# A hybrid decoder step on one core: split waits, moved copies, an earlier reload and a regrouped end

## The chip, the cores and the metric
The kernel runs on one core of one Trainium2 chip. A core has TensorE (PE, matrix products), VectorE (DVE), ScalarE (ACT), GpSimd (POOL), and SyncE (SP), which here only issues DMA transfers; 16 DMA engines move the data. The metric is the device time of one execution in microseconds (us).

## The reference
One layer of a decoder for 320 tokens: 256 of a prompt and 64 of 8 samples of 8. All is float32.

```python
h = rms_norm(x, g_mix)
proj = h @ w_in                  # u | qkv | z | beta | a | gate_a | gate_b
y_s5 = gelu(s5(u))               # diagonal complex state space, scan over positions
y_s5 = y_s5 * sigmoid(y_s5 @ w_glu + b_glu)
y_dn = gated_delta(conv(qkv), beta, a, S0) ; norm ; * silu(z)
mix = sigmoid(gate_a) * (y_s5 @ w_a) + sigmoid(gate_b) * (y_dn @ w_b)
x = x + mix @ w_out
x = x + (silu(h2 @ w_gate) * (h2 @ w_up)) @ w_down       # h2 = rms_norm(x, g_ffn)
x = x + (p @ w_ple) * sigmoid(h3 @ w_ple_gate)           # h3 = rms_norm(x, g_ple)
y = rms_norm(x, g_final)         # y_prompt 256 x 2048, y_sample 8 x 8 x 2048
```

D is 2048, the S5 and DeltaNet widths are 1024, FFN 5632, the per-layer embedding p has 256 columns. The states of the convolution, the DeltaNet and the S5 branch are outputs too.

## The kernel before
Activations lie transposed, features on the 128 partitions and the 320 tokens along the row. A weight is cut into units of 512 rows by 256 columns (512 KB). SP loads unit n into slot n mod 4 of the ring `raw` as soon as unit n-4 has been split; SP's queue is in order, so a load or store placed between two units waits for its own conditions with all later loads behind it. ScalarE rounds the unit to `whi` (L959), VectorE takes the rest `wlo` = raw - whi (L1410); the activations have halves of the same kind (`xhi`/`xlo`, for the S5 branch `yhi`/`ylo`). TensorE multiplies a unit in three parts of 8 products each: whi with the high half, whi with the low half, wlo with the high half (`unit`, L2172), into the accumulator `pg`.

What runs between the units is written out by hand. `schedule()` is a list of slots, each with side tasks and a number of units. Every engine walks the same list: TensorE does a slot's side tasks and then its units; ScalarE and VectorE split the slot's units first and then do the side tasks. So on ScalarE and VectorE a side task of one slot stands ahead of the splits of the next. Their PSUM results go to two regions, `side_a` and `side_b`, used in turn as `side_fills()` lists them.

Side tasks named below: `sq` h multiplies a sample's query and key with head h's old state (VectorE uses the result at L1900, `vb`); `vn` and `o` 2 belong to the sample's chunk; the decay of a head's state is L1660 (`st` times `egl`, 128x1024); `su` adds to the states; `ysplit` makes `yhi` on ScalarE (L1220) and `ylo` on VectorE (L1926). `masked_values(h)` makes 8 masked copies `vnb` on ScalarE (within L962) which `su` needs. After the gates come the products of the glu (`glu`, 4 pairs of 2 units), then w_a and w_b with the gates fetched back by SP from DRAM (`gr`, L590), then w_out.

The input x is written to DRAM early (`scratch_x`) and loaded back to `xt` (2560 KB, L621) ahead of w_out's residual addition. MIX_UNITS is the number of units before w_out.

Last comes the per-layer embedding: 8 rounds of four units of w_ple_gate and one of w_ple (256 rows), into `side_a` and `side_b` by turns (`emb` i). After round 7: gate, sigmoid (L1348), product `fmd` (L2092), addition to `xt` (L2100), squares (L1358), their sum in `acc`, and the column sums of `acc` with ones (`norm` 3, L2198) which give `invt`, one number per token. TensorE turns `xg` (xt times the norm's weight) to token-major by products with `ident` (L2646, L2660) in five groups: `fin` 0 0, `turned_0`, `turned_1`, `fin` 1 1 and `fin` 2 (the samples, two column halves on 2 x 64 partitions). ScalarE (L1389) and VectorE (L2141) scale them by `invt` into `yo` and `yo2`, and SP stores them (L655 to L664).

ScalarE's own DMA queue carries 11 small transfers in the first slot (`const`): four norm weights as 16 rows of 128, two vectors as 8 rows, one row, the convolution's 96 rows, and three tables of 32 rows:

```python
src = w if w is g_final else w[0]
act.dma_start(par1n[at:at + KD, :], src.rearrange("(k p) -> k p", p=P)).then_inc(sem("par_landed"), 16)
...
act.dma_start(par1n[ONW:ONW + 1, :], onorm_w).then_inc(sem("par_landed"), 16)
```

Of the kernel before, what the change touches and what calls it, by code (L numbers as in the profile page):

```python
# [22 lines left out]
P = 128  # L23
# [116 lines left out]
def schedule():  # L140
# [108 lines left out]
def hybrid_layer(nc, x_prompt, x_sample, state_conv, state_delta, state_s5_re, state_s5_im, p_prompt, p_sample,  # L249
# [26 lines left out]
    with ExitStack() as ctx:  # L276
# [189 lines left out]
        xg = zo.take("xg", [P, KD, NPR])  # L466
        xgs = zo.take("xgs", [P, KD // 2, 2, NSM])

        scr_x = nc.dram_tensor("scratch_x", [P, KD, N], F32, kind="Internal").ap()
# [68 lines left out]
        def _(sp):  # L538
# [54 lines left out]
            for n, (p, j) in enumerate(units):  # L593
# [24 lines left out]
            sp.wait_ge(sem("x_stored"), 16)  # L618
            sp.wait_ge(sem("on_ready"), H // 2)
            sp.wait_ge(sem("st_stored"), 16 * H)  # L620
            sp.dma_start(xt[:], scr_x).then_inc(sem("xt_landed"), 16)  # L621

# [328 lines left out]
        def _(act):  # L951
# [80 lines left out]
            def side(key):  # L1032
# [168 lines left out]
                elif what == "o":  # L1201
                    c0, n = CHUNKS[a[0]]
                    wait_filled(act, key)
                    drain(act.activation(hsplit(qt[:, :, c0:c0 + n]), hview(key, a[0]), ACT.Copy), key)
                    if a[0] == 2:
                        wait_drained(act, ("vn", 2))
                        masked_values(0)
                        masked_values(1)
                elif what == "sq":
                    if a[0] == 0:  # L1210
                        wait_filled(act, ("s", 1))
                    wait_filled(act, key)
                    copy(vn[NSM:P, a[0], :], ps(key)[NSM:P, 0, 0:P]).then_inc(sem("qs_ready"), 1)
                elif what == "su" and a[0] + 2 < H:
                    masked_values(a[0] + 2)
# [134 lines left out]
            def final_x(i):  # L1350
                act.wait_ge(sem("xf_ready"), i + 1)
                if i < 7:
                    finish(xt, i + 24, i, None)
                else:
                    act.wait_ge(sem("acc_added"), 31)
# [9 lines left out]
            for i in range(8):  # L1365
# [35 lines left out]
        def _(dve):  # L1401
# [260 lines left out]
            def side(key):  # L1662
# [231 lines left out]
                elif what == "sq":  # L1894
                    h = a[0]
                    if h == 0:
# [190 lines left out]
            def ple_out(i):  # L2087
# [5 lines left out]
                wait_drained(dve, key)  # L2093
                if i < 7:
                    xs = xt[:, 2 * i:2 * i + 2, :]
                    dve.tensor_tensor(xs, xs, fmd[:], ALU.add).then_inc(sem("xf_ready"), 1)
                    dve.wait_ge(sem("xf_ready"), i + 1)
                else:
                    for m in range(2):
                        dve.tensor_tensor(xt[:, 14 + m, :], xt[:, 14 + m, :], fmd[:, m, :], ALU.add).then_inc(sem("xf_ready"), 1)  # L2100

            dve.wait_ge(sem("phi_ready"), 1)
            dve.tensor_tensor(plo[:], pf[:], phi[:].bitcast(F32), ALU.subtract).then_inc(sem("plo_ready"), 1)
            for i in range(8):
# [15 lines left out]
                else:  # L2120
# [6 lines left out]
                    s(4)  # L2127
            ple_gate_out(7)
            ple_out(7)
# [20 lines left out]
        def _(pe):  # L2150
# [10 lines left out]
            def unit(u, r, par, k0, nk, first, last, hi, lo, out=None, lows_ready=None):  # L2161
# [12 lines left out]
                ins.then_inc(multiplied, 1)  # L2174

            def token_transposes(out, cols, src):

# [4 lines left out]
            def norm(i):  # L2182
                key = ("norm", i)
                if i == 3:
                    pe.wait_ge(sem("last_added"), 3)
                elif i:
# [9 lines left out]
                if i == 3:  # L2196
                    for c in range(3):
                        ins = pe.matmul(out[:, 1, c:c + 1], acc[:, c * P:(c + 1) * P], ones[:, 0:1], start=True, stop=True)  # L2198
                end(ins, key)
# [350 lines left out]
            for s, (sides, us) in enumerate(slots):  # L2550
                for key in sides:
                    side(key)
                for n in [units.index(u) for u in us]:
# [77 lines left out]
            for i in range(KD // 2):  # L2631
# [6 lines left out]
                out = begin(key)  # L2638
                unit(u + 4, (5 * i + 4) % RING, None, 0, PLE // P, True, True, phi, plo, out)
                if i == 0:  # L2640
# [13 lines left out]
            pe.wait_ge(evacuated, PLE_P + 8)  # L2654
            turned(pg[:, 1], 0, 1).then_inc(sem("turned_1"), 1)
# [35 lines left out]
```

## Time and profile before

| | |
|---|---|
| median of 3 runs | 1991.0 us (1990.8 to 1991.43) |
| the profiled execution's own time | 1990.88 us |
| its span in the profile | 1989.1 us |
| TensorE busy | 1969.3 us, 99% |
| VectorE, ScalarE, GpSimd busy | 57%, 41%, 16% |
| TensorE's granted clock | 0.999 of full speed |
| share of TensorE in the chain that ended last | 93% |

The span runs from the first to the last recorded event and is 1.8 us shorter than the time. Times in the rows are us from the span's start. A row of the timeline merges instructions of one line that follow each other (x8: eight of them); the bracket at its end is the idle time of that engine just before it and what ended it.

### The profile page before, as it was taken

What the parts mean: (1) busy time and instruction counts of PE and PEld (TensorE: products, weight loads), DVE (VectorE), ACT (ScalarE), POOL (GpSimd) and SP (SyncE); (2) the same over time, 40 slices, a digit from 0 to 9 for tenths busy, and PEclk for the clock granted to TensorE, in tenths of its full rate; (3) what the DMA queues carried; (4) which work ended last, traced back from release to release, by engine and by line L of the source; (5) the groups of instructions that cost most, each with busy time, mean ns of one, the idle gap of its engine ahead of it and who ended that gap; (6) DMA issues with size and microseconds to landing.
All of it is one profiled execution on the core that took longest, in us unless ns stands there. A gap on an engine that the chain in (4) does not pass through costs nothing.

```text
span 1989.1 us, 38799 instructions
## 1 busy us (share of the span) xinstructions
PE 1969.3 (99%) x15613; PEld 1934.8 (97%) x15613; DVE 1126.5 (57%) x1409; ACT 814.4 (41%) x1069; POOL 316.8 (16%) x378
## 2 busy tenths in 40 slices
PE   8999999999999999999999999999999999999998
PEld 8999999899999899999999999999999999999997
DVE  7799997873646767544444444334444444444554
ACT  7343336643434563344333333333333333333543
POOL 3955443000003200011000000000000000001111
PEclk9999999999999999999999999999999999999999
DMA  9544445545437486644544444444444444444442
GB/s 232 177 136 129 131 137 151 161 124 147 120 110 217 146 261 221 216 148 145 151 148 150 151 151 149 148 148 154 148 148 150 151 151 144 149 143 158 144 148 101
DMA packets 300261, 308.07 MB, mean 155 GB/s; under 512 B 24949, under 2 KB 290822, under 8 KB 299890
## 3 DMA queue, kind: packets, MB, share of 16 engines
q1 hardware_dynamic: 296800, 296.76, 48.5%
q0 software_dynamic: 2928, 9.54, 1.7%
q8 instruction: 85, 1.39, 0.3%
q14 instruction: 30, 0.25, 0.0%
q10 hardware_dynamic: 418, 0.12, 0.0%
HBM read 289.24 MB, written 17.14 MB: 154 GB/s over the span
## 4 chain that ended last, share of the span: by engine, by line
PE 93%; DVE 4%; ACT 1%; DMA 1%; issue 1%; ACTq 0%; SPq 0%; DVEq 0%
PE pg L2172 86%; DVE cacc L1754 2%; DVE wlo L1410 1%; PE side_a L2214 1%; PE side_a L2205 1%; DMA raw<-in_w_out 1%; ACT whi L959 1%; PE side_a L2519 0%; PE side_a L2172 0%; DMA par2n<-in_conv_w 0%; PE side_a L2538 0%; PE side_b L2172 0%; PE side_b L2205 0%; ACT vnb L962 0%; PE side_a L2436 0%
## 5 line engine op out<-in xcount | busy, mean ns | idle before, releaser
L1410 DVE TENSOR_TENSOR wlo<-raw,whi 128x1024 fp32r<-128x1024 f32 (+1 forms) x528 | 650.2, 1239 | 639.6 <-ACT whi L959 637.8
L959 ACT ACTIVATE whi<-raw 128x1024 fp32r<-128x1024 f32 (+1 forms) x528 | 544.6, 1039 | 896.3 <-PE pg L2172 835.7
L2172 PE MATMUL pg<-xhi,whi 128*128 128x320 f32 x2816 | 478.4, 312 | 1.5 <-ACT whi L959 1.4
L2172 PE MATMUL pg<-xhi,wlo 128*128 128x320 f32 x2816 | 470.6, 309 | 1.2 <-DVE wlo L1410 1.2
L2172 PE MATMUL pg<-xlo,whi 128*128 128x320 f32 x2816 | 470.3, 309 | 1.1 <-DVE xlo L1417 1.1
L2172 PEld LDWEIGHTS pg<-xhi,whi 128*128 128x128 f32 x2816 | 424.3, 188 | 10.8 <-issue 7.3
L2172 PEld LDWEIGHTS pg<-xhi,wlo 128*128 128x128 f32 x2816 | 427.3, 188 | 2.4 <-DVE wlo L1410 2.2
L2172 PEld LDWEIGHTS pg<-xlo,whi 128*128 128x128 f32 x2816 | 427.5, 188 | 1.4 <-DVE xlo L1417 1.4
L929 POOL TENSOR_TENSOR fsi<-fsg,inv 128x640 f32<-128x640 f32 x22 | 43.3, 1970 | 706.6 <-ACT fsg L1293 706.6
L2172 PE MATMUL pg<-mhi,wlo 128*128 128x320 f32 x704 | 118.9, 309 | 0.0
L2172 PE MATMUL pg<-mlo,whi 128*128 128x320 f32 x704 | 118.8, 309 | 0.0
L2172 PE MATMUL pg<-mhi,whi 128*128 128x320 f32 x704 | 118.8, 309 | 0.0
L2172 PEld LDWEIGHTS pg<-mhi,whi 128*128 128x128 f32 x704 | 107.3, 188 | 0.0
L2172 PEld LDWEIGHTS pg<-mhi,wlo 128*128 128x128 f32 x704 | 107.3, 188 | 0.0
L2172 PEld LDWEIGHTS pg<-mlo,whi 128*128 128x128 f32 x704 | 107.3, 188 | 0.0
L914 POOL TENSOR_TENSOR acc<-acc,sq 128x320 f32<-128x320 f32 x23 | 23.3, 1014 | 393.8 <-ACT sq L967 393.8
L676 POOL TENSOR_TENSOR pt<-ta,tb 128x256 f32<-128x256 f32 x64 | 70.5, 1121 | 73.1 <-DVE gg L1633 71.8
L1009 ACT ACTIVATE stg<-g 128x640 f32<-128x640 f32 x20 | 14.8, 740 | 73.4 <-DVE g L1455 73.4
L2172 PE MATMUL pg<-mxhi,whi 128*128 128x320 f32 x256 | 42.8, 309 | 0.5 <-ACT whi L959 0.5
L2172 PE MATMUL pg<-mxhi,wlo 128*128 128x320 f32 x256 | 42.7, 309 | 0.0
L2172 PE MATMUL pg<-mxlo,whi 128*128 128x320 f32 x256 | 42.6, 308 | 0.0
L2172 PEld LDWEIGHTS pg<-mxhi,whi 128*128 128x128 f32 x256 | 38.8, 188 | 0.7 <-issue 0.7
(495 smaller groups left out, 1709.8 us busy)
## 6 DMA issues: line engine op xcount, KB each, us to landing
raw<-in_w_in SPq DMA_DIRECT2D x144, 512.0 KB, 4.1
raw<-in_w_gate SPq DMA_DIRECT2D x88, 512.0 KB, 3.5
raw<-in_w_up SPq DMA_DIRECT2D x88, 512.0 KB, 3.5
raw<-in_w_down SPq DMA_DIRECT2D x80, 512.0 KB, 3.5
raw<-in_w_out SPq DMA_DIRECT2D x32, 512.0 KB, 3.5
raw<-in_w_ple_gate SPq DMA_DIRECT2D x32, 512.0 KB, 3.5
raw<-in_w_a SPq DMA_DIRECT2D x16, 512.0 KB, 5.7
raw<-in_w_b SPq DMA_DIRECT2D x16, 512.0 KB, 4.2
```

Of the source, the lines that this page charges most:

```text
L676: ins = pool.tensor_tensor(out, a, b, op)
L914: pool.tensor_tensor(acc[:, 0:N], acc[:, 0:N], sq[:, 0, :], ALU.add).then_inc(sem("pool_steps"), 1)
L929: pool.tensor_tensor(fsi[:], fsg[:], inv[:].unsqueeze(1).broadcast_to([P, 2, N]), ALU.mult).then_inc(sem("fsi_ready"), 1)
L959: act.activation(whi[:, r, 0:nk, :], raw[:, r, 0:nk, :], ACT.Copy).then_inc(w_hi, 1)
L1009: act.activation(stg[:, n % 2], g1[:], ACT.Silu if kind == "z" else ACT.Sigmoid).then_inc(sem("stage_written"), 1)
L1410: dve.tensor_tensor(wlo[:, r, 0:nk, :], raw[:, r, 0:nk, :], whi[:, r, 0:nk, :].bitcast(F32), ALU.subtract).then_inc(w_lo, 1)
L1754: ins = dve.scalar_tensor_tensor(out=s, in0=qkv[:, t, j:j + NCV], scalar=w, in1=s, op0=ALU.mult, op1=ALU.add)
L2172: ins = pe.matmul(out[:, m, 0:N], w[:, r, k, m * P:(m + 1) * P], a[:, k0 + k, :], start=first and k == 0 and part == 0, stop=last and k == ...
L2205: ins = pe.matmul(out[0:rows or P, h // 4, (h % 4) * n:(h % 4) * n + n], lhs(h), rhs(h), start=True, stop=True)
L2214: ins = pe.matmul(out[r, h // 4, (h % 4) * size:(h % 4 + 1) * size], lhs(h, r), rhs(h, r), start=True, stop=True)
```

## The change
1. The first glu product waits for `yhi` before its first part and for `ylo` only before its second; before, for `ylo` ahead of all.
2. The decays of heads 0 to 5 move from the tasks `sq` 0 to 5 to `sq` 2 to 7.
3. The masked copies of heads 0 and 1 leave the task `o` 2 for a new task `mask`, one slot later.
4. The reload of `xt` is issued after the load of unit MIX_UNITS - 8 instead of after the last.
5. At the end the last round goes by halves of 128 columns: the product (`last_unit`), the gate, the sigmoid, `fmd` and the addition. The squares go to a tile of their own, `sqx`; TensorE sums `acc` and both halves of `sqx` (9 products instead of 3), VectorE's two additions to `acc` go. `norm` 3 stands ahead of `turned_0` instead of behind it.
6. The first store of y is cut in two (256 KB each), the two stores of the samples become one.

The core of the diff:

```diff
             for i in range(0, H, 2):
-                slot([], 1)
+                slot([("mask",)] * (i == 0), 1)
                 slot([("su", i), ("su", i + 1)], 1)
...
+                if n == MIX_UNITS - 2 * RING:
+                    sp.wait_ge(sem("x_stored"), 16)
+                    sp.wait_ge(sem("on_ready"), H // 2)
+                    sp.wait_ge(sem("st_stored"), 16 * H)
+                    sp.dma_start(xt[:], scr_x).then_inc(sem("xt_landed"), 16)
                 while fetched < 20 and due[fetched] == n + 1:
...
+            sp.wait_ge(sem("y_first"), 1)
+            sp.dma_start(y_prompt[0, 0:P, 0:D // 4], yo[:, 0, 0:D // 4]).then_inc(sem("y_stored"), 16)
             wait_drained(sp, ("fin", 0, 0))
-            sp.dma_start(y_prompt[0, 0:P, first], yo[:, 0, first]).then_inc(sem("y_stored"), 16)
+            sp.dma_start(y_prompt[0, 0:P, D // 4:D // 2], yo[:, 0, D // 4:D // 2]).then_inc(sem("y_stored"), 16)
...
             wait_drained(sp, ("fin", 2))
-            for k, cols in enumerate((first, second)):
-                sp.dma_start(y_sample.rearrange("b l d -> (b l) d")[:, cols], yo2[NSM * k:NSM * k + NSM, :]).then_inc(sem("y_stored"), 16)
+            sp.dma_start(y_sample.rearrange("b l (k c) -> k (b l) c", k=2), yo2[:]).then_inc(sem("y_stored"), 16)
...
-                        act.activation(sq[:, m, :], xt[:, 14 + m, :], ACT.Square).then_inc(sem("last_squares"), 1)
+                        act.activation(sqx[:, m, 0:N], xt[:, 14 + m, :], ACT.Square).then_inc(sem("last_squares"), 1)
...
-            gate_sig(7)
+            for m in range(2):
+                act.wait_ge(sem("last_gate"), m + 1)
+                act.activation(fsg[:, m, :], fg1[:, m, :], ACT.Sigmoid).then_inc(sem("last_sig"), 1)
...
-            drain(tokens_out(yo[:, 0, 0:D // 2], ps(key)[:], 0), key)
+            for k in range(2):
+                cols = slice(k * D // 4, (k + 1) * D // 4)
+                ins = act.activation(yo[:, 0, cols], ps(key)[:, k, :], ACT.Copy, scale=invt[:, 0:1])
+                ins.then_inc(sem("y_first"), 1) if k == 0 else drain(ins, key)
...
-                    if h < 6:
-                        decay_state(h)
+                    if h >= 2:
+                        decay_state(h - 2)
...
+            dve.tensor_copy(acc[:, N:3 * P], acc[:, NPR:N]).then_inc(sem("sums_doubled"), 1)
+            key = ("emb", 7)
             for m in range(2):
-                dve.wait_ge(sem("last_squares"), m + 1)
-                dve.tensor_tensor(acc[:, 0:N], acc[:, 0:N], sq[:, m, :], ALU.add).then_inc(sem("last_added"), 1)
-                dve.wait_ge(sem("last_added"), m + 1)
-            dve.tensor_copy(acc[:, N:3 * P], acc[:, NPR:N]).then_inc(sem("last_added"), 1)
+                dve.wait_ge(sem("last_emb"), m + 1)
+                dve.wait_ge(sem("last_sig"), m + 1)
+                ins = dve.tensor_tensor(fmd[:, m, :], ps(key)[:, m, 0:N], fsg[:, m, :], ALU.mult)
...
+                last = xt[:, 14 + m, NPR:N]
+                dve.tensor_tensor(sqx[:, m, N:3 * P], last, last, ALU.mult).then_inc(sem("squares_doubled"), 1)
...
+                        pe.matmul(out[:, 1, c:c + 1], acc[:, c * P:(c + 1) * P], ones[:, 0:1], start=c == 0, stop=False)
+                    for m in range(2):
+                        pe.wait_ge(sem("last_squares"), m + 1)
+                        pe.wait_ge(sem("squares_doubled"), m + 1)
+                        for c in range(3):
+                            ins = pe.matmul(out[:, 1, c:c + 1], sqx[:, m, c * P:(c + 1) * P], ones[:, 0:1],
+                                            start=False, stop=m == 1 and c == 2)
...
                     if kind == "glu" and i == 0:
-                        pe.wait_ge(sem("ylo_ready"), j + 1)
+                        pe.wait_ge(sem("yhi_ready"), j + 1)
+
+                        def lows_ready(n=j + 1):
+                            pe.wait_ge(sem("ylo_ready"), n)
...
             end(turned(begin(("fin", 0, 0)), 0, 0), ("fin", 0, 0))
+            norm(3)
             pe.wait_ge(evacuated, PLE_P + 7)
             turned(pg[:, 0], 1, 0).then_inc(sem("turned_0"), 1)
-            norm(3)
```

VectorE's instructions from the first two `sq` to the first glu units, in the kernel before (`g_132` is a gate, `st_156` and `st_157` the states of heads 0 and 1):

```order
L1410 TENSOR_TENSOR wlo<-raw,whi 128x1024
L1900 SCALAR_TENSOR_TENSOR vb<-side_a,nbe,vb 64x128
L1660 TENSOR_TENSOR st_156<-st_156,egl 128x1024
L1900 SCALAR_TENSOR_TENSOR vb<-side_b,nbe,vb 64x128
L1660 TENSOR_TENSOR st_157<-st_157,egl 128x1024
L1410 TENSOR_TENSOR wlo<-raw,whi 128x1024
L1926 TENSOR_TENSOR ylo<-yt,yhi 128x1280 x2
```

The same stretch in the changed kernel, to the next two `sq`:

```order
L1416 TENSOR_TENSOR wlo<-raw,whi 128x1024
L1906 SCALAR_TENSOR_TENSOR vb<-side_a,nbe,vb 64x128
L1906 SCALAR_TENSOR_TENSOR vb<-side_b,nbe,vb 64x128
L1416 TENSOR_TENSOR wlo<-raw,whi 128x1024
L1932 TENSOR_TENSOR ylo<-yt,yhi 128x1280 x2
L1416 TENSOR_TENSOR wlo<-raw,whi 128x1024
L1461 TENSOR_TENSOR g_132<-pg,inv 128x640
L1906 SCALAR_TENSOR_TENSOR vb<-side_a,nbe,vb 64x128
L1666 TENSOR_TENSOR st_156<-st_156,egl 128x1024
L1906 SCALAR_TENSOR_TENSOR vb<-side_b,nbe,vb 64x128
L1666 TENSOR_TENSOR st_157<-st_157,egl 128x1024
```

The two decays (L1660, now L1666) move from between the two `vb` of `sq` 0 and 1, ahead of `wlo` and `ylo`, to those of `sq` 2 and 3, behind both.

ScalarE's instructions around the task `o` 2 in the kernel before (`qt` is the copy that `o` 2 makes):

```order
L959 ACTIVATE whi<-raw 128x1024
L1012 ACTIVATE g_132<-g_132 128x640
L1204 ACTIVATE qt<-side_b 128x8x64
L962 ACTIVATE vnb<-vn,seqm 64x128 x8
L959 ACTIVATE whi<-raw 128x1024 x2
L1012 ACTIVATE g_132<-g_132 128x640
L962 ACTIVATE vnb<-vn,seqm 64x128 x8
```

And in the changed kernel:

```order
L961 ACTIVATE whi<-raw 128x1024
L1014 ACTIVATE g_132<-g_132 128x640
L1206 ACTIVATE qt<-side_b 128x8x64
L961 ACTIVATE whi<-raw 128x1024
L964 ACTIVATE vnb<-vn,seqm 64x128 x8
L961 ACTIVATE whi<-raw 128x1024
L1014 ACTIVATE g_132<-g_132 128x640
L964 ACTIVATE vnb<-vn,seqm 64x128 x8
```

Of the two splits `whi` that stood behind the first eight `vnb`, one now stands ahead of them.

SP's last instructions in the kernel before, the stores of y (`yo_184` is the tile yo2):

```order
L655 DMA out_y_prompt<-yo 128x1024
L657 DMA out_y_prompt<-yo 128x1024
L659 DMA out_y_prompt<-yo 128x1024
L661 DMA out_y_prompt<-yo 128x1024
L664 DMA out_y_sample<-yo_184 64x1024 x2
```

And in the changed kernel:

```order
L656 DMA out_y_prompt<-yo 128x512
L658 DMA out_y_prompt<-yo 128x512
L660 DMA out_y_prompt<-yo 128x1024
L662 DMA out_y_prompt<-yo 128x1024
L664 DMA out_y_prompt<-yo 128x1024
L666 DMA out_y_sample<-yo_184 2x64x1024
```

Five stores of the prompt stand where four stood, and one of 2 x 64 rows where two of 64 rows stood.

## Rows read from the trace of the kernel before

**Rows 1.** The page, busy time of each engine over the whole span
```profile
...
PE 1969.3 (99%) x15613; PEld 1934.8 (97%) x15613; DVE 1126.5 (57%) x1409; ACT 814.4 (41%) x1069; POOL 316.8 (16%) x378
...
```

**Rows 2.** Waits of TensorE over the span: total us, times, longest
```profile
...
PE pg L2172 <- ACT whi L959: 3.3, 5, 1.2
...
```

**Rows 3.** Timeline, first glu product: start, us, engine, line, operation, [idle before <-releaser]
```profile
...
635.58 1.21 DVE L1660 TENSOR_TENSOR st<-st,egl 128x1024 f32<-128x1024 f32 x1
...
636.86 1.33 PE L2172 MATMUL pg<-xlo,whi 128*128 128x320 f32 x8
636.97 1.21 DVE L1660 TENSOR_TENSOR st<-st,egl 128x1024 f32<-128x1024 f32 x1
636.98 2.42 ACT L1220 ACTIVATE yhi<-yt 128x1280 fp32r<-128x1280 f32 x2
...
638.03 1.34 PE L2172 MATMUL pg<-xhi,wlo 128*128 128x320 f32 x8
...
639.24 2.88 DVE L1926 TENSOR_TENSOR ylo<-yt,yhi 128x1280 fp32r<-128x1280 f32 x2
...
640.82 0.96 PE L2172 MATMUL pg<-yhi,whi 128*128 128x320 f32 x5 [1.45 <-issue]
```

**Rows 4.** Timeline, masked copies and the splits behind them
```profile
...
676.75 2.57 ACT L962 ACTIVATE vnb<-vn,seqm 64x128 f32<-64x128 f32 x8
...
679.34 2.01 ACT L959 ACTIVATE whi<-raw 128x1024 fp32r<-128x1024 f32 x2
...
680.54 0.68 PE L2172 MATMUL pg<-ghi,whi 128*128 128x320 f32 x3 [1.25 <-ACT whi L959]
```

**Rows 5.** Timeline, second of these splits
```profile
...
689.31 0.96 PE L2172 MATMUL pg<-ghi,whi 128*128 128x320 f32 x5 [0.22 <-ACT whi L959]
...
```

**Rows 6.** Timeline, SP's last loads of w_b, the reload, the start of w_out
```profile
...
783.48 0.39 SPq L544 DMA_DIRECT2D raw<-in_w_b  x1
...
790.53 0.37 SPq L621 DMA_DIRECT2D xt<-scratch_x  x1
...
799.59 1.34 PE L2172 MATMUL pg<-dhi,whi 128*128 128x320 f32 x8
...
802.55 1.06 ACT L959 ACTIVATE whi<-raw 128x1024 fp32r<-128x1024 f32 x1 [12.20 <-DMA raw<-in_w_out]
...
803.76 1.42 PE L2172 MATMUL pg<-mxhi,whi 128*128 128x320 f32 x8 [0.49 <-ACT whi L959]
...
```

**Rows 7.** Timeline of VectorE, after the sixth sq
```profile
...
673.44 1.23 DVE L1410 TENSOR_TENSOR wlo<-raw,whi 128x1024 fp32r<-128x1024 f32 x1 [2.68 <-ACT whi L959]
...
```

**Rows 8.** Busy us (instructions) by engine, TensorE's clock, DMA, in one stretch
```profile
...
680.50:694.10 13.60, 13.34 (x89) 11.19 (x89) 12.86 (x15) 9.99 (x22) 1.83 (x2) 1.00 0.60 185
...
```

**Rows 9.** DMA issues around the reload: KB each, median us to landing
```profile
...
raw<-in_w_out SPq DMA_DIRECT2D x7, 512.0 KB, 11.2
...
```

**Rows 10.** Timeline of the end, to the first store of y
```profile
...
1974.24 0.82 DVE L2092 TENSOR_TENSOR fmd<-side_a,fsg 128x640 f32<-128x640 f32 x1 [0.94 <-PE side_a L2172]
...
1977.63 0.74 PEld L2198 LDWEIGHTS side_a<-ones,acc 128*128 128x128 f32 x6 [1.92 <-DVE acc L2135]
1977.63 0.83 PE L2198 MATMUL side_a<-ones,acc 128*128 128x1 f32 x6 [1.68 <-DVE acc L2135]
...
1978.32 1.07 PE L2646 MATMUL pg<-ident,xg 128*128 128x128 f32 x8
...
1979.00 1.11 ACT L1389 ACTIVATE yo<-side_b,invt 128x1024 f32<-128x1024 f32 x1 [0.24 <-DVE invt L2137]
...
1980.14 0.36 SPq L655 DMA_DIRECT2D out_y_prompt<-yo  x1
...
```

**Rows 11.** DMA of the end, 40 slices of 0.5 us from 1970
```profile
...
GB/s 0 0 0 0 0 0 0 0 0 0 0 0 0 0 0 0 0 33 0 0 0 8 426 401 402 393 401 418 410 385 418 401 320 205 180 385 90 0 0 0
DMA packets 737, 2.64 MB, mean 132 GB/s; under 512 B 96, under 2 KB 96, under 8 KB 736
...
```

**Rows 12.** The page, DMA of ScalarE's queue: packets, MB, share
```profile
...
q10 hardware_dynamic: 418, 0.12, 0.0%
...
```

More of the change, by code:

```diff
@@ L467, in hybrid_layer @@
         xgs = zo.take("xgs", [P, KD // 2, 2, NSM])
+        sqx = zo.take("sqx", [P, 2, 3 * P])
         scr_x = nc.dram_tensor("scratch_x", [P, KD, N], F32, kind="Internal").ap()
@@ L615, in _ @@
                     fetched += 1
[L618 to L621, printed above, removed]
             with sp.Fori(0, 4) as it:
@@ L1204, in side @@
                     drain(act.activation(hsplit(qt[:, :, c0:c0 + n]), hview(key, a[0]), ACT.Copy), key)
[L1205 to L1208, printed above, removed]
                 elif what == "sq":
@@ L1213, in side @@
                     copy(vn[NSM:P, a[0], :], ps(key)[NSM:P, 0, 0:P]).then_inc(sem("qs_ready"), 1)
+                elif what == "mask":
+                    wait_drained(act, ("vn", 2))
+                    masked_values(0)
+                    masked_values(1)
                 elif what == "su" and a[0] + 2 < H:
@@ L1350, in final_x @@
             def final_x(i):
-                act.wait_ge(sem("xf_ready"), i + 1)
                 if i < 7:
+                    act.wait_ge(sem("xf_ready"), i + 1)
                     finish(xt, i + 24, i, None)
                 else:
-                    act.wait_ge(sem("acc_added"), 31)
                     for m in range(2):
                         act.wait_ge(sem("xf_ready"), 8 + m)
-                        act.activation(sq[:, m, :], xt[:, 14 + m, :], ACT.Square).then_inc(sem("last_squares"), 1)
+                        act.activation(sqx[:, m, 0:N], xt[:, 14 + m, :], ACT.Square).then_inc(sem("last_squares"), 1)
                 for m in range(2):
@@ L2093, in ple_out @@
                 wait_drained(dve, key)
[L2094 to L2100, printed above, removed]
+                xs = xt[:, 2 * i:2 * i + 2, :]
+                dve.tensor_tensor(xs, xs, fmd[:], ALU.add).then_inc(sem("xf_ready"), 1)
+                dve.wait_ge(sem("xf_ready"), i + 1)
             dve.wait_ge(sem("phi_ready"), 1)
@@ L2127, in _ @@
                     s(4)
-            ple_gate_out(7)
-            ple_out(7)
+            dve.wait_ge(multiplied, PLE_U + 5 * 7 + 4)
+            for m in range(2):
+                ins = dve.tensor_tensor(fg1[:, m, :], pg[:, 1, m, 0:N], inv[:], ALU.mult)
+                ins.then_inc(sem("last_gate"), 1)
             dve.wait_ge(sem("acc_added"), 31)
+            dve.tensor_copy(acc[:, N:3 * P], acc[:, NPR:N]).then_inc(sem("sums_doubled"), 1)
+            key = ("emb", 7)
             for m in range(2):
-                dve.wait_ge(sem("last_squares"), m + 1)
-                dve.tensor_tensor(acc[:, 0:N], acc[:, 0:N], sq[:, m, :], ALU.add).then_inc(sem("last_added"), 1)
-                dve.wait_ge(sem("last_added"), m + 1)
-            dve.tensor_copy(acc[:, N:3 * P], acc[:, NPR:N]).then_inc(sem("last_added"), 1)
+                dve.wait_ge(sem("last_emb"), m + 1)
+                dve.wait_ge(sem("last_sig"), m + 1)
+                ins = dve.tensor_tensor(fmd[:, m, :], ps(key)[:, m, 0:N], fsg[:, m, :], ALU.mult)
+                if m == 0:
+                    o.link(ins)
+                else:
+                    drain(ins, key)
+                    wait_drained(dve, key)
+                dve.tensor_tensor(xt[:, 14 + m, :], xt[:, 14 + m, :], fmd[:, m, :], ALU.add).then_inc(sem("xf_ready"), 1)
+                dve.wait_ge(sem("xf_ready"), 8 + m)
+                last = xt[:, 14 + m, NPR:N]
+                dve.tensor_tensor(sqx[:, m, N:3 * P], last, last, ALU.mult).then_inc(sem("squares_doubled"), 1)
             wait_drained(dve, ("norm", 3))
@@ L2174, in unit, with last_unit @@
                 ins.then_inc(multiplied, 1)
+            def last_unit(u, r, out):
+                pe.wait_ge(w_lo, u + 1)
+                for m in range(2):
+                    for part, (w, a) in enumerate(((whi, phi), (whi, plo), (wlo, phi))):
+                        for k in range(PLE // P):
+                            ins = pe.matmul(out[:, m, 0:N], w[:, r, k, m * P:(m + 1) * P], a[:, k, :],
+                                            start=part == 0 and k == 0, stop=part == 2 and k == PLE // P - 1)
+                    ins.then_inc(sem("last_emb"), 1)
             def token_transposes(out, cols, src):
@@ L2184, in norm @@
                 if i == 3:
-                    pe.wait_ge(sem("last_added"), 3)
+                    pe.wait_ge(sem("sums_doubled"), 1)
                 elif i:
@@ L2197, in norm @@
                     for c in range(3):
-                        ins = pe.matmul(out[:, 1, c:c + 1], acc[:, c * P:(c + 1) * P], ones[:, 0:1], start=True, stop=True)
+                        pe.matmul(out[:, 1, c:c + 1], acc[:, c * P:(c + 1) * P], ones[:, 0:1], start=c == 0, stop=False)
+                    for m in range(2):
+                        pe.wait_ge(sem("last_squares"), m + 1)
[3 more added lines that the diff above has]
+                                            start=False, stop=m == 1 and c == 2)
                 end(ins, key)
@@ L2638, in _ @@
                 out = begin(key)
-                unit(u + 4, (5 * i + 4) % RING, None, 0, PLE // P, True, True, phi, plo, out)
+                if i < KD // 2 - 1:
+                    unit(u + 4, (5 * i + 4) % RING, None, 0, PLE // P, True, True, phi, plo, out)
+                else:
+                    last_unit(u + 4, (5 * i + 4) % RING, out)
                 if i == 0:
@@ L2649, in _ @@
             end(turned(begin(("fin", 0, 0)), 0, 0), ("fin", 0, 0))
+            norm(3)
             pe.wait_ge(evacuated, PLE_P + 7)
             turned(pg[:, 0], 1, 0).then_inc(sem("turned_0"), 1)
-            norm(3)
             pe.wait_ge(sem("xg_ready"), KD)
-            pe.wait_ge(evacuated, PLE_P + 8)
+            pe.wait_ge(sem("last_gate"), 2)
             turned(pg[:, 1], 0, 1).then_inc(sem("turned_1"), 1)
```

## The prediction
> **What bounds the kernel now.** I read the page first: TensorE is busy 99% of the span [rows 1], so outside the last 20 us only its waits can be won. Then the list of TensorE's waits: the lines of the weight multiplications wait 3.3 us on ScalarE's splits of the weights, in five waits [rows 2]. Then the timeline around each wait, where a row's bracket gives the idle time and who ended it. Last the end of the run, by timeline and by DMA traffic, since there the chain leaves TensorE for the stores of y.
>
> How a wait is read: a row of 8 matmuls shows 1.33 or 1.34 us, but the next row begins 1.17 us after it (636.86 and 638.03 [rows 3]); the ends are modelled. So a stall is the bracket plus 0.17 us.
>
> **Part 1: four stalls in the middle.**
> (a) At 640.82 TensorE starts the first glu unit with a bracket of 1.45, a stall of 1.62 us [rows 3]. It waits for the low halves of y: VectorE ran two decays (635.58 and 636.97, 1.21 us each), the split of a weight and then two low halves, 639.24 + 2.88. The high halves by ScalarE were done at 636.98 + 2.42 = 639.40, of which the first half stands at 638.2. With the change part 0 needs the highs alone, and the decays are gone from here, so the lows start some 2.4 us earlier and the first stands at about 639.7, when part 1 is wanted at 639.20 + 1.17 = 640.37: 0.6 us to spare. Gain 1.62.
> (b) At 680.54 the bracket is 1.25 [rows 4]: ScalarE makes 8 masked copies (676.75, 2.57 us) before the split of the weight at 679.34. In the new order the split goes first and is done near 678 at the latest, before TensorE wants it at 679.13. Gain 1.25 + 0.17 = 1.42, taken as 1.41 from the start times.
> (c) At 689.31 the same queue of ScalarE is still late by 0.22 + 0.17 = 0.39 [rows 5]; with the queue ahead of it 1.4 us earlier, it goes. Gain 0.39.
> (d) At 803.76 a bracket of 0.49, 0.66 us in all (0.65 by start times): the split at 802.55 had waited for the first unit of w_out [rows 6], which SP issues behind the 2560 KB reload of x, at 790.53 [rows 6]. Moved to about 758.8, the reload is over long before. Gain 0.65.
> Sum 1.62 + 1.41 + 0.39 + 0.65 = 4.07 us.
>
> What hides the moved work. The six decays now stand behind the later state products; two more of them fall ahead of 673.44, 2.42 us, and VectorE is idle for 2.68 us right there [rows 7], so nothing waits for them. The masked copies, one slot later, stand ahead of work in a stretch where VectorE is busy 12.86 of 13.60 us and ScalarE 9.99 [rows 8]: that is the thin place. If (a) and (c) come back there as other waits, 1.41 + 0.65 = 2.06 stays. The reload is queued ahead of the loads of w_b: the last of these is issued at 783.48 and its unit starts on TensorE at 799.59 [rows 6], 16.1 us, less 1.06 for the split 15.0. A load behind the reload landed after 11.2 us (the median of the seven w_out loads in that window [rows 9]). 11.2 is less than 15.0, so I cost the move at nothing. If that cover goes, the difference is paid once. The middle thus gives 2.06 to 4.07; I take 4.07, as each of the four has its own cause removed.
>
> **Part 2: the sums before the transposes.** Before, the last sums start on TensorE at 1977.63, after a wait of 1.68 on VectorE's additions [rows 10]. These additions go. The nine column products, two instructions each, can start once the last product is drained: 1974.24 + 0.82 for VectorE's pass [rows 10] and about 0.2 for the signals, 1975.25. Six instructions took 0.74 us of weight loads and 1.37 us from the first to the scaling (1977.63 to 1979.00); 18 take 3 x 0.74 = 2.22, and 1.37 - 0.74 = 0.63 follows. The scaling starts at 1975.25 + 2.22 + 0.63 = 1978.10 in place of 1979.00. The first store waits for half of ScalarE's 1.11 us: 1978.10 + 0.56 + 0.03 = 1978.69 in place of 1980.14 [rows 10], 1.45 earlier. All other transposes now follow the sums on TensorE, one of them more than before, but each makes 512 KB ready in 1.07 us of matmuls [rows 10], where the stores take 1.29 for as much (at the 406 GB/s below), so they don't hold the stream. The end of the range of this step: if the six extra products hide altogether in the wait, 1.48 us earlier still; if the start of the stores does not move, 1.45 later.
>
> **Part 3: the stores.** In the ten full slices of 0.5 us from 1981.0 the kernel writes 406 GB/s on the mean [rows 11], that is 25.3 GB/s for each of 16 engines. The first bytes came 0.85 us after the first store's issue. The prompt's 2.097 MB then run from 1978.69 + 0.85 = 1979.54 for 5.17 us, to 1984.7.
>
> The sample's store is another matter. It was two transfers of 64 rows; it is now one whose destination has the halves outermost, 2 x 64 x 1024. How a transfer is spread over engines the rows show for ScalarE's queue: 418 packets [rows 12]. Its eleven transfers (four of 16 rows, two of 8, one of 1, one of 96 and three of 32) have 273 data rows. The rest, 145, are the closing 4-byte packets, which the end of the run shows as 96 for six stores, 16 each [rows 11]. If all closed on 16 engines they would be 176 and the row 449. 145 is 64 + 16 + 1 + 16 + 48, a transfer of 8 rows closing on 8 engines and one of 1 on 1. So the leading size deals a transfer out. I read from this that a leading size of 2 puts the store on 2 engines. Each then has 64 rows of 4 KB, 262 KB, at 25.3 GB/s 10.35 us. Behind the prompt's share that ends at 1984.7 + 10.35 = 1995.05. Interleaved with it the two engines have the same bytes to move, so the order does not matter. Before, the last slice with traffic is the one from 1988.0 to 1988.5, at 90 GB/s [rows 11]: the end is between 1988.1 and 1988.5, and I take 1988.4. Loss 6.65 us.
>
> The Trainium skill bears on this in "DMA: Bandwidth & Descriptors", section "Why a DMA increments its semaphore by 16 and not by 1": the number of engines is the largest, up to 16, that divides the slowest dimension other than 1 of both access patterns. For 2 at the destination and 128 at the source that is 2; the 418 packets agree with it, and no row of before shows a nested pattern such as this one. By the rule the end stands at 1995.05; if the source's 128 rows alone counted, it would be rival A's.
>
> **The sum.** The profiled execution took 1990.88, its span 1989.1. -4.07 + 6.65 = +2.58, so 1993.5; the median of the runs is 1991.0, and on it 1993.6 is what I give. Ends: -4.07 + 6.65 - 1.48 = +1.1, or 1992.0; -2.06 + 6.65 + 1.45 = +6.0, or 1997.0.
>
> **Rivals.**
> A. The sample's store is spread over 16 engines all the same. For it: its source has 128 rows, and none of ScalarE's transfers shows which side's leading size counts where the two differ. Against it: the small leading sizes did count there [rows 12]. Then it ends 524 KB at 406 GB/s after 1984.7, at 1986.0, 2.4 before 1988.4; with 4.07 that is -6.5: 1984.6. Chance 0.09.
> B. The early reload makes the loads of w_b late. Its place is the ring's loads on SP between 758 and 783; its price starts when such a load takes more than 15.0 us to land. For it: 2560 KB then stand ahead of them in the same queue. Against it: the 11.2 above [rows 9]. At twice that, TensorE waits 22.4 - 15.0 = 7.4 and the time is 1993.6 + 7.4 + 0.65 = 2001.6. Slower; chance 0.03.
> C. The stalls come back through VectorE at 680 to 694, where 0.74 us of 13.60 is free. Then 2.06 of the 4.07 stays, and the time is 1995.6. Chance 0.08, slower.
> D. The two engines move the rows at half pace, as the slices of 205 and 180 GB/s do near the end of before though the engines show busy [rows 11]: 20.7 in place of 10.35, and 2004. Chance 0.04, slower.
>
> **How the numbers follow.** Two tenths of a per cent, what a measurement of this kernel can tell from none, is 4.0 us: under 1987.0 is faster, over 1995.0 slower. The forecast has 0.76; its own range 1992.0 to 1997.0 has some 0.09 beyond 1995.0. Faster is A with a little of a smaller tail, 0.10. Slower is 0.09 + 0.03 + 0.08 + 0.04 = 0.24. The rest, 0.66, is no change. The range of 8 in 10 holds the forecast's own and C: 1991.5 to 1997.5; A, B and D, 0.16, are left out.
>
> **What would show it.** Right: no row of TensorE with a bracket over 0.2 at the four places, the reload issued near 759, the first store of y near 1974.6 on the new clock (4.07 earlier than 1978.69). At the end about ten us in which the DMA traffic is near 50 GB/s; 82 small packets, 5 x 16 + 2, in place of 96; a landing of 11 to 12 us for the sample's store. Wrong: traffic near 400 GB/s until the last byte (A), brackets with the DMA of w_b behind them (B), or brackets on VectorE's splits after 680 (C).

## The result, and the profile after

| | before | changed |
|---|---|---|
| median | 1991.43 us (15 runs, 1990.8 to 1993.3) | 1995.28 us (15 runs, 1994.8 to 1995.7) |
| ratio | | 1.0018, 95% interval 1.0011 to 1.0025 |
| the profiled execution | 1990.88 us, span 1989.1 | 1995.05 us, span 1993.3 |

The change made the kernel 3.85 us slower by the medians, 4.17 by the profiled executions; 2.58 was forecast, with 1991.5 to 1997.5 as the range.

Two things pull against each other: the waits in the middle went, and the end grew a tail of slow DMA traffic. First the middle. The page of the changed kernel (busy time of each engine over the span) still has TensorE at 99% [rows 1]; in the list of TensorE's waits, the line that stood first among its weight products is smaller:

```profile
...
PE 1971.7 (99%) x15625; PEld 1938.4 (97%) x15625; DVE 1126.0 (56%) x1411; ACT 814.9 (41%) x1071; POOL 309.4 (16%) x378
...
```
```profile
...
PE pg L2186 <- ACT whi L961: 0.7, 2, 0.5
...
```

0.7 us in two waits stand where 3.3 in five stood [rows 2]. Three of the five are those of [rows 4, 5, 6], 1.96 us, and they are gone; the other two lie in the first 25 us, ahead of anything that the change touches. The timeline around the first glu product (start, us, engine, line, operation, and in brackets the idle time before):

```profile
...
636.66 2.42 ACT L1222 ACTIVATE yhi<-yt 128x1280 fp32r<-128x1280 f32 x2
...
637.71 1.34 PE L2186 MATMUL pg<-xhi,wlo 128*128 128x320 f32 x8
637.95 2.89 DVE L1932 TENSOR_TENSOR ylo<-yt,yhi 128x1280 fp32r<-128x1280 f32 x2
...
638.88 1.33 PE L2186 MATMUL pg<-yhi,whi 128*128 128x320 f32 x8
...
```

TensorE's rows follow each other at 1.17 us with no bracket; the stall of 1.62 us [rows 3] is gone. VectorE starts the low halves (L1932) at 637.95, with no decay ahead of them. The next two places, where the masked copies (L964) now come behind a split (L961):

```profile
...
674.74 1.05 ACT L961 ACTIVATE whi<-raw 128x1024 fp32r<-128x1024 f32 x1
...
675.69 2.57 ACT L964 ACTIVATE vnb<-vn,seqm 64x128 f32<-64x128 f32 x8
...
675.96 1.34 PE L2186 MATMUL pg<-yhi,wlo 128*128 128x320 f32 x8
...
677.13 1.34 PE L2186 MATMUL pg<-ghi,whi 128*128 128x320 f32 x8
...
685.44 1.34 PE L2186 MATMUL pg<-ghi,whi 128*128 128x320 f32 x8
...
```

And w_out, with the reload (L618) issued at 754.93 and the last load of w_b at 779.50:

```profile
...
754.93 0.45 SPq L618 DMA_DIRECT2D xt<-scratch_x  x1
...
779.50 0.39 SPq L545 DMA_DIRECT2D raw<-in_w_b  x1
...
797.96 1.33 PE L2186 MATMUL pg<-dhi,wlo 128*128 128x320 f32 x8
...
799.13 1.34 PE L2186 MATMUL pg<-mxhi,whi 128*128 128x320 f32 x8
...
```

None of 677.13, 685.44 and 799.13 has a bracket, where 1.25, 0.22 and 0.49 stood [rows 4, 5, 6].

The end. Timeline of the changed kernel from the first product of the last unit of w_ple:

```profile
...
1968.00 0.46 PE L2196 MATMUL side_a<-phi,whi 128*128 128x320 f32 x2
...
1970.49 0.48 DVE L2140 TENSOR_TENSOR fmd<-side_a,fsg 128x320 f32<-128x320 f32 x1
...
1971.12 0.80 PE L2222 MATMUL side_a<-ones,acc 128*128 128x1 f32 x6 [0.32 <-DVE fmd L2140]
...
1971.79 1.48 PE L2227 MATMUL side_a<-ones,sqx 128*128 128x1 f32 x12
...
1973.12 3.50 PE L2682 MATMUL pg<-ident,xg 128*128 128x128 f32 x16
...
1973.81 1.27 ACT L1397 ACTIVATE yo<-side_b,invt 128x512 f32<-128x512 f32 x2 [0.24 <-DVE invt L2151]
1974.52 0.36 SPq L656 DMA_DIRECT2D out_y_prompt<-yo  x1
...
1978.96 0.33 SPq L664 DMA_DIRECT2D out_y_prompt<-yo  x1
1979.66 0.64 SPq L666 DMA_DIRECT2D out_y_sample<-yo  x1
```

The same first product in the kernel before:

```profile
...
1972.27 0.75 PE L2172 MATMUL side_a<-phi,whi 128*128 128x320 f32 x4
...
```

1972.27 became 1968.00, 4.27 us earlier. The scaling of y starts at 1973.81 and the first store goes at 1974.52, 5.62 earlier than the 1980.14 of before [rows 10]. But the 16 transposes behind the sums take 3.50 us. The granted clock by stretch (stretch, length, busy time of PE, PEld, DVE, ACT, POOL with instructions, clock, DMA share, GB/s):

```profile
...
1971.10:1973.10 2.00, 1.98 (x18) 2.00 (x19) 0.63 (x2) 1.64 (x5) 0.44 (x1) 1.00 0.04 8
1973.10:1974.90 1.80, 1.80 (x11) 1.80 (x11) 0.18 (x1) 1.35 (x3) 0.00 (x0) 0.56 0.00 0
1974.90:1976.40 1.50, 1.50 (x9) 1.50 (x8) 1.28 (x1) 0.17 (x1) 0.00 (x0) 0.50 0.68 254
1976.40:1977.40 1.00, 1.00 (x10) 1.00 (x9) 0.00 (x0) 0.74 (x1) 0.00 (x0) 0.84 0.64 246
...
```

From 1974.9 to 1976.4 the clock is 0.50 of full speed, the level of 1.2 GHz; it fell early in the stretch before (0.56), behind 2.0 us in which TensorE did one-column products. The experiments below show that these products are not needed for such a fall. Then the DMA traffic from 1966 on, 40 slices of 0.7 us, the small packets, and the sample's store:

```profile
...
GB/s 0 0 0 0 0 0 0 0 0 23 0 0 0 217 395 173 404 310 386 404 410 310 35 35 12 47 47 47 53 53 53 53 53 53 53 53 53 41 0 0
DMA packets 851, 2.64 MB, mean 94 GB/s; under 512 B 82, under 2 KB 82, under 8 KB 850
...
out_y_sample<-yo SPq DMA_DIRECT2D x1, 512.0 KB
```

The prompt runs at up to 410 GB/s until about 1981.3; then comes a tail of eleven us, 12 to 35 GB/s in its first slices and 47 to 53 in the rest. 82 packets are under 512 B where 96 were [rows 11]: five stores close on 16 engines and one on 2. A finer view of the same tail, slices of 0.33 us from 1980; its first line is the busy share of the 16 DMA engines in tenths:

```profile
...
DMA  9996120130011111111111111111111111111000
GB/s 407 431 394 259 49 49 0 49 49 0 25 49 25 49 49 49 49 62 49 49 62 49 49 49 62 49 49 62 49 49 49 62 49 49 62 49 49 25 0 0
...
```

Most slices have 49 GB/s at a busy share of one tenth: two engines of 16, at 25 GB/s each. From 1982.0 to 1984.3 slices of 0 and 25 stand among them, where the two engines worked for longer on some of the sample's first rows.

### The profile page after: what moved, and what is told of

Same layout as the page of the kernel before. It is cut to its first block, busy times and chain, and to the rows that moved or that the text cites. A ratio compares the mean times of both kernels' runs of the same rounds, so it can differ in the third digit from the quotient of the medians.

```text
span 1993.3 us, 38827 instructions
## 1 busy us (share of the span) xinstructions
PE 1971.7 (99%) x15625; PEld 1938.4 (97%) x15625; DVE 1126.0 (56%) x1411; ACT 814.9 (41%) x1071; POOL 309.4 (16%) x378
## 4 chain that ended last, share of the span: by engine, by line
PE 94%; DVE 3%; ACT 0%; issue 0%; DMA 0%; ACTq 0%; DVEq 0%
PE pg L2186 88%; DVE cacc L1760 2%; DVE wlo L1416 1%; PE side_a L2244 1%; PE side_a L2235 1%; PE side_a L2549 0%; PE side_a L2186 0%; DMA par2n<-in_conv_w 0%; ACT whi L961 0%; PE side_a L2568 0%; PE side_b L2508 0%; PE side_b L2186 0%; PE side_b L2235 0%; PE side_a L2526 0%; PE side_a L2466 0%
## 5 line engine op out<-in xcount | busy, mean ns | idle before, releaser
L961 ACT ACTIVATE whi<-raw 128x1024 fp32r<-128x1024 f32 (+1 forms) x528 | 544.7, 1039 | 896.3 <-PE pg L2186 838.8
L931 POOL TENSOR_TENSOR fsi<-fsg,inv 128x640 f32<-128x640 f32 x22 | 43.3, 1970 | 706.6 <-ACT fsg L1295 706.6
L2186 PEld LDWEIGHTS pg<-mxhi,wlo 128*128 128x128 f32 x256 | 39.1, 188 | 0.0
```

The lines of the kernel that those rows point to most:

```text
L931: pool.tensor_tensor(fsi[:], fsg[:], inv[:].unsqueeze(1).broadcast_to([P, 2, N]), ALU.mult).then_inc(sem("fsi_ready"), 1)
L961: act.activation(whi[:, r, 0:nk, :], raw[:, r, 0:nk, :], ACT.Copy).then_inc(w_hi, 1)
L2186: ins = pe.matmul(out[:, m, 0:N], w[:, r, k, m * P:(m + 1) * P], a[:, k0 + k, :], start=first and k == 0 and part == 0, stop=last and k == ...
```

## The experiments

**Two stores again (e1_two_stores).** The changed kernel with one part undone:

```diff
-sp.dma_start(y_sample.rearrange("b l (k c) -> k (b l) c", k=2), yo2[:]).then_inc(sem("y_stored"), 16)
+for k, cols in enumerate((first, second)):
+    sp.dma_start(y_sample.rearrange("b l d -> (b l) d")[:, cols], yo2[NSM * k:NSM * k + NSM, :]).then_inc(sem("y_stored"), 16)
...
```

> The changed kernel with the sample's store undone alone: two stores of 64 rows as before, all else as changed. Theory (a leading size of 2 puts the one store on 2 DMA engines): in the changed kernel the prompt's bytes end near 1981.3 and the sample's near 1992.5; on 16 engines the sample takes some 1.3 to 2.1 us, so the end comes about 9 us earlier: 1986.2 (1985.3 to 1987.0), with 96 + 16 small packets (seven stores) and traffic near 400 GB/s to the last byte. Rival (rows of this destination are slow to write however they are dealt out, or the loss comes from the reordered sums): 1994 to 1995.5.

Measured: 1986.14 us (8 runs, 1985.5 to 1986.9), 0.9973 of before (0.9963 to 0.9984). Its DMA traffic from 1970, slices of 0.4 us:

```profile
...
GB/s 0 0 0 0 0 0 0 0 41 0 0 0 0 0 256 364 389 425 420 389 379 440 410 399 215 430 389 348 266 195 184 215 379 62 0 0 0 0 0 0
DMA packets 881, 2.64 MB, mean 165 GB/s; under 512 B 112, under 2 KB 112, under 8 KB 880
...
```

The tail at 50 GB/s is gone and 112 small packets are 7 x 16. So 9.1 us of the changed kernel's time hang on this one store, and all the rest of the change together is worth 5.2 us to the good (1991.33 for the kernel before, measured beside it).

**One store in the kernel before (e2_before_one_store).** The same part done alone, the reverse of the diff above.

> The kernel before with one part of the change alone: the two stores of the sample become the one of 2 x 64 rows. Theory (2 engines): the sample's bytes follow the prompt's, which end near 1986.2, and take the 11.1 us they took in the changed kernel instead of some 2.2: 2000.3 (1999.3 to 2001.3). Rival (the loss needs the new end around it, its sums or the clock): 1991 to 1992.

Measured: 2000.22 us (5 runs, 1999.8 to 2001.1) against 1991.33, 1.0045 (1.0031 to 1.0058). Slices of 0.73 us from 1970:

```profile
...
GB/s 0 0 0 0 0 0 0 0 0 0 0 0 0 0 0 254 412 390 401 412 413 390 243 23 45 17 40 45 56 51 51 56 51 51 56 51 51 56 0 0
DMA packets 706, 2.62 MB, mean 90 GB/s; under 512 B 66, under 2 KB 66, under 8 KB 706
...
```

66 small packets are 4 x 16 + 2, and the traffic falls from about 400 to about 50 GB/s as soon as the prompt is out, with none of the new end around it. The loss is 8.9 us, so it does not need the new sums. On the clock e2 alone says nothing, for it was at 0.50 here too, from 1980.2 to 1982.5:

```profile
...
1978.49 1.07 PE L2645 MATMUL pg<-ident,xg 128*128 128x128 f32 x8
...
1979.40 1.73 PE L2645 MATMUL side_a<-ident,xg 128*128 128x128 f32 x8
...
1980.92 1.91 PE L2659 MATMUL side_b<-ident,xgs 128*128 128x128 f32 x8
...
```

But e1 above has that fall with two stores and no such loss, and the slow tail runs when TensorE has no product left: here its last row ends at 1982.8 and the tail begins near 1986.3. With that the rival falls.

**The parts in the middle, each alone on the kernel before.** First the split wait and the decays together (m1), then the mask task (m2), then the reload (m3):

```diff
 # m1
-    pe.wait_ge(sem("ylo_ready"), j + 1)
+    pe.wait_ge(sem("yhi_ready"), j + 1)
+    def lows_ready(n=j + 1):
+        pe.wait_ge(sem("ylo_ready"), n)
...
-    if h < 6:
-        decay_state(h)
+    if h >= 2:
+        decay_state(h - 2)
 # m2
-    slot([], 1)
+    slot([("mask",)] * (i == 0), 1)
...
-    masked_values(0)
-    masked_values(1)
...
+elif what == "mask":
...
+    masked_values(0)
+    masked_values(1)
 # m3
+    if n == MIX_UNITS - 2 * RING:
...
+        sp.dma_start(xt[:], scr_x).then_inc(sem("xt_landed"), 16)
...
-sp.dma_start(xt[:], scr_x).then_inc(sem("xt_landed"), 16)
```

> The kernel before with the first glu product's split wait and the moved decays alone. Theory: the stall of 1.62 us ahead of the first glu unit goes and the other three (1.41, 0.39, 0.65) stay; time 1.6 lower. Rival (the moved decays come back as a wait on VectorE some units later): a new bracket with VectorE behind it between 660 and 700, time less than 1.0 lower.

Measured: 1989.74 us against 1992.02 on that chip, 0.9989 (0.9980 to 0.9998). TensorE's waits (us in all, times, longest):

```profile
...
PE pg L2172 <- ACT whi L959: 1.9, 3, 1.2
...
```

The first glu unit shows no bracket, and none with VectorE behind it came between 660 and 700. The three waits for ScalarE's splits that are left are those of the other parts (679.06, 687.82 and 802.20). The time is 2.3 us lower where 1.6 was expected; the interval, 0.4 to 4.0, holds both, so the trace decides and not the time.

> The kernel before with the masked copies moved alone. Theory: the stalls of 1.41 (near 680) and 0.39 (near 689) go, since ScalarE's split is ahead of the copies; time 1.8 lower. Rival (the copies, one slot later, make the state products or the next splits wait): a new bracket between 680 and 700, time less than 1.0 lower.

Measured: 1989.55 us, 0.9988 (0.9979 to 0.9998).

```profile
...
PE pg L2172 <- issue: 1.5, 1, 1.5
...
PE pg L2172 <- ACT whi L959: 0.4, 1, 0.4
```

The longest wait for a split, 1.2 [rows 2], is gone, so is the 0.22 of [rows 5], and no bracket came in their place between 680 and 700. The one at the glu, here put down to issue at 1.5, stands, and so does the one ahead of w_out, 0.4. The time is 2.5 us lower where 1.8 was expected, inside the interval again.

> The kernel before with the reload of x moved ahead of the last loads of w_b alone. Theory: the loads of w_b have 15 us and need some 11, so the one stall of 0.65 us ahead of w_out goes and none comes; time 0.65 lower. Rival (the loads behind the reload land too late): brackets with a DMA of w_b behind them near 775 to 800, time 0 to 7 higher.

Measured: 1991.42 us, 0.9997 (0.9988 to 1.0006): too small for the time to tell. The trace tells: the first product of w_out (`mxhi`, `whi`) follows without a bracket, and no weight product behind the one at 690.08 has one.

```profile
...
802.74 1.34 PE L2173 MATMUL pg<-dhi,wlo 128*128 128x320 f32 x8
803.91 1.34 PE L2173 MATMUL pg<-mxhi,whi 128*128 128x320 f32 x8
...
```

**What the first glu stall was made of (m4, m5).** The two halves of m1 apart.

> The kernel before with the split wait of the first glu product alone, the decays where they were. Theory (two causes feed one stall): the first part starts at once, and the second waits for the first low half, which VectorE ends at 639.24 + 1.44 = 640.68 in place of 640.37: 0.3 to 0.4 of the 1.62 us stays, 1.2 to 1.3 go. Rival (the split wait takes all of it, the decays did not matter): no bracket of TensorE between 638 and 642.

```profile
...
640.39 1.34 PE L2172 MATMUL pg<-yhi,whi 128*128 128x320 f32 x8
640.42 2.88 DVE L1926 TENSOR_TENSOR ylo<-yt,yhi 128x1280 fp32r<-128x1280 f32 x2
...
641.95 1.44 PE L2172 MATMUL pg<-ylo,whi 128*128 128x320 f32 x8 [0.23 <-DVE ylo L1926]
...
```

The first part starts at once; its second part begins at 641.95 - 640.39 = 1.56 us after it, where 1.17 is the pace: 0.39 stays. Time 1990.51 us against 1991.97 on that chip, 0.9994 (0.9984 to 1.0003), not to be told from no change. The rival, that the split wait takes all of the stall, falls.

> The kernel before with the moved decays alone, the first glu product still waiting for the low halves ahead of its first part. Theory: the low halves start behind the first high half (638.2) in place of 639.24, so the first ends near 639.65 and TensorE starts near 639.8 in place of 640.82: 1.0 of the 1.62 us go, 0.6 stays. Rival (the decays alone take the stall away): no bracket over 0.2 there.

```profile
...
639.01 1.34 PE L2172 MATMUL pg<-xhi,wlo 128*128 128x320 f32 x8
639.25 2.90 DVE L1926 TENSOR_TENSOR ylo<-yt,yhi 128x1280 fp32r<-128x1280 f32 x2
...
640.85 1.41 PE L2172 MATMUL pg<-yhi,whi 128*128 128x320 f32 x8 [0.50 <-issue]
...
```

640.85 - 639.01 - 1.17 = 0.67 stays, so the decays alone don't take it all either. Time 1990.74 us, 0.9993 (0.9984 to 1.0003). Each half takes most of the stall, only both take it all: 1.23 and 0.95 add to more than 1.62 because they free the same wait.

**The fall of the clock (e3, e4).** Both have the two stores of the first experiment. e3 moves the call `norm(3)` back behind `turned_0`; e4 widens the products:

```diff
-pe.matmul(out[:, 1, c:c + 1], acc[:, c * P:(c + 1) * P], ones[:, 0:1], ...)
+pe.matmul(out[:, 1, c * P:(c + 1) * P], acc[:, c * P:(c + 1) * P], ones[:], ...)
```

> The changed kernel with two stores of the sample, and the last sums put back behind the first transposes into the accumulator (the order of before). In the changed kernel TensorE's granted clock is 0.50 from 1974.9 to 1976.4, after 2.0 us of one-column products. Theory (those products, with the wait ahead of them, bring the clock down): with 8 transposes between the last products and the sums the time of low work gets shorter and the clock stays at 1.0; the sums end about 0.9 us later, the transposes behind them take 1.05 for 8; against the kernel with two stores alone the time is 0.2 lower to 0.4 higher. Rival (the clock falls after the last weights in any case): the transposes behind the sums again take 1.6 to 1.75 for 8, and the time is 0.7 to 1.5 higher.

Measured: 1986.41 us (9 runs), against 1986.14 of the first experiment on the same chip. The granted clock stays at 1.00:

```profile
...
1973.10:1974.90 1.80, 1.80 (x18) 1.80 (x19) 0.00 (x0) 0.99 (x3) 0.00 (x0) 1.00 0.03 9
1974.90:1976.40 1.50, 1.50 (x15) 1.31 (x12) 1.39 (x2) 1.26 (x4) 0.00 (x0) 1.00 0.00 0
...
```

> The changed kernel with two stores of the sample, and the 9 products of the last sums made with 128 columns of ones instead of one (the same sums, in 128 equal columns): the order and the number of products stay. Theory (one-column products leave TensorE's array idle, and the clock falls): the clock stays at 1.0 through the transposes, 16 of them take 2.1 in place of 3.5 us, and the prompt's bytes end about 0.7 us earlier: 1985.5, if the wide products take no longer than the weight loads do now (2.2 us for all); at up to 0.26 each for 18 it is 2.5 us later at the scaling, and the time 1986 to 1988. Rival (the clock falls whatever the products' width): 16 transposes take 3.5 us again, 1986.2 or later.

Measured: 1986.06 us (7 runs). The wide products take 1.50 us for twelve, the narrow ones 1.48, and the 16 transposes 1.91:

```profile
...
1972.50 1.50 PE L2228 MATMUL side_a<-ones,sqx 128*128 128x128 f32 x12
...
1973.84 1.91 PE L2683 MATMUL pg<-ident,xg 128*128 128x128 f32 x16
...
```

In clock and transposes both came out as the theory has it; the time of e4 did not fall with them (1986.06, where 1985.5 was expected). And neither shows the theory. The profile of e1 has a clock of 0.50, that of e5, the next experiment, whose end is the same instruction for instruction, one of 1.00 (the stretch from 1974.9 in the one and in the other):

```profile
...
1974.90:1976.40 1.50, 1.50 (x9) 1.50 (x9) 1.04 (x1) 0.94 (x2) 0.00 (x0) 0.50 0.44 165
...
```
```profile
...
1974.90:1976.40 1.50, 1.50 (x16) 1.50 (x15) 1.28 (x1) 1.47 (x3) 0.00 (x0) 1.00 0.28 102
...
```

Nor does a fall need the nine narrow products. The kernels e2, m1, m2 and m4 have the end of before, with three column sums behind a wait of 1.68 us, and in their profiles the clock is at 0.50 during the last transposes (1.57 to 1.92 us for 8 of them, as in the rows of e2 above); before, m3 and m5 have the same end, and there it stays at 1.00 until TensorE is done. So with the same end the clock falls in one execution and not in another, and one profile each of e3 and e4 at 1.00 may be luck. What brings it down is not shown.

With two stores the fall costs little. The profiled executions of e1, with it, and e5, without, took 1985.92 and 1985.89; the first store of y went at 1974.87 in e1 and at 1975.11 in e5, so e1 lost some 0.25 us behind it, in this one pair. The medians, 1986.14, 1986.41, 1986.06 and 1986.18 for e1, e3, e4 and e5, lie within 0.35 of each other; of the executions without a profile only the mean clock is on record.

**The sample's slow rows (e5_sample_touched).** This one, too, has the two stores of the first experiment. The added transfer writes 512 bytes of each of the sample's 64 rows long before the end:

```diff
...
+sp.dma_start(y_sample.rearrange("b l d -> (b l) d")[:, 0:P], ones[0:NSM, :]).then_inc(sem("y_touched"), 16)
...
```

> The changed kernel with two stores of the sample, and 64 pieces of 512 bytes of ones written to y_sample behind the reload of x, some 1200 us before the end (written over by the last stores). In each run the first 4 KB rows of the sample take 0.2 to 0.7 us where all others take 0.16, wherever in time they fall. Theory (the first write to that tensor is what is slow): the slow rows go, the last slices stay near 400 GB/s, time 0.7 lower than with two stores alone. Rival (they are slow whenever they are written, or because they are last): no change within 0.2.

Measured: 1986.18 us (8 runs). Slices of 0.4 us from 1970:

```profile
...
GB/s 0 0 0 0 0 0 0 0 41 0 0 0 0 0 31 353 389 399 425 389 410 389 430 389 410 399 440 379 297 205 164 297 358 0 0 0 0 0 0 0
...
```

297, 205, 164 and 297 GB/s near the end, as in the first experiment (266, 195, 184, 215). The theory of the first write falls, as far as 512 bytes of each row can tell; what slows these rows stays open.

## Why the prediction was right, and where it fell short

Part 1 was right by its own steps. Each of the four stalls went, and each by the cause that was named (m1 to m5). The forecast gain was 4.07. The last round begins 4.27 earlier, but 0.30 of that is a stall near 542 in the profile of before which the change doesn't touch (between 0 and 0.86 in the other profiles, whose code is the same there); 3.97 is left. That this comes within 0.1 is partly luck. Matched product by product, the start times move by some 4.4 us at the four places, as the first products behind a stall also came a little slower than the bracket plus 0.17 counts; and some 0.4 is given back between 804 and 930, where w_out's parts follow each other at 1.176 us (835.57 to 844.98 in eight) and before at 1.170 (842.50 to 848.35 in five). The slower pace is also in the profiles of m1, m3 and m4 and not in those of m2, m5 and e2, so no single edit goes with it; its cause stays open. The cover held: in the changed kernel the load of w_b behind the reload cost no bracket (rival B), and VectorE's full stretch brought none (rival C).

Part 2 was right to 0.2 us. On the new clock the scaling was to start at 1978.10 - 4.07 = 1974.03 and did at 1973.81, the first store at 1974.62 and went at 1974.52. The nine products take nearly what was worked out: 0.74 and 1.42 us of weight loads, 2.16 in place of 2.22. No run has the new end alone; its worth is read from the profiles, the first store 5.62 us earlier where the last round began 4.27 earlier.

Part 3 was right in its mechanism: two engines, 25 GB/s each, shown by e1 and e2 from both sides. Rival A, a sample on 16 engines, is what e1 made with two stores: 1986.1, 1.5 us above its 1984.6. The size of the loss was the weak step: 6.65 us in the sum, where the profiled executions give 4.17 + 4.07 = 8.24. The 1.59 us of difference lie in two terms, both too small; the stated range was wide enough to hold them:
- "for 5.17 us, to 1984.7" for the prompt, 1980.6 on the new clock; its traffic ends near 1981.3, 0.7 later. The transposes were priced at 1.07 us for 8 [rows 10] and took 1.75 at the lower clock, so the third store went 1.82 us behind the first (1974.52 and 1976.34); in e5, the same end at 1.00, it went 1.10 behind (1975.11 and 1976.21). I had taken the clock from one profile of before, where it stayed at 1.00 through a wait of 1.68 us; m1, m2, m4 and e2 show that with this same end it may fall as well. That the 0.7 come from the clock is read from these two profiles; it wasn't tried by itself with the sample on two engines.
- "262 KB, at 25.3 GB/s 10.35 us" for the sample; from 1981.3 to 1992.5 it took 11.2. The rows of the end [rows 11] had shown slices of 320, 205 and 180 GB/s where the sample began. Taken as rival D, half pace throughout, they got a chance of 0.04; they are a slow start after which the pace returns, in every profile of this case, and belonged into the main sum with some 0.9 us.

The Trainium skill's rule ("DMA: Bandwidth & Descriptors", section "Why a DMA increments its semaphore by 16 and not by 1"), untried here before, is now shown for a nested pattern: 82 and 66 small packets, each with one store closing on 2.

## What to carry to other kernels

Count the engines a transfer is dealt over before merging two into one: here one issue fewer on SP cost 9 us, as the merged pattern had its two halves outermost, and the number of closing packets in the trace tells it. Where several edits free one wait, price the wait and not the edits, and look for what is late next (here 0.39 and 0.67 us of 1.62). Read the clock from more than one profile before a price is built on it. Of the versions measured, the one to keep is the changed kernel with the sample in two stores, 1986.14 us, 5.2 below before and 9.1 below the change as it was made; e3, e4 and e5, built on it, are within 0.3 of it.

## What the runs showed of the hardware that was not expected

- TensorE's clock fell to 0.50 while it was still at work near the end in six of twelve profiles: the changed kernel, e1, e2, m1, m2 and m4. It did not in before, m3 and m5, which have the end of e2, m1, m2 and m4, nor in e5, which has that of e1, nor in e3 and e4. So the same instructions came with either clock. The Trainium skill, "TensorE: Matmul & The Clock Gate", section "Part 1: The HAM clock gate", says that the window of the monitor behind the clock is free-running and does not reset when a kernel starts; that would fit, and no run here was made to show it.
- The first rows of the sample's store ran slower than the rest (slices of some 160 to 320 GB/s on 16 engines, 0 to 25 among those of 49 on 2) in all twelve profiles, at whatever time they came, also when part of each row had been written before.
